# First layer's shift and scale columns on ScalarE, and the rope angles in three parts

## The reference

```python
c_act = jax.nn.silu(c)
shift, scale, gate = jnp.split(c_act @ mod_w[i] + mod_b[i], 3, axis=-1)
h = _rms_norm(x, norm_g[i]) * (1.0 + scale[:, None, :]) + shift[:, None, :]
q, k, v, g = jnp.split(h @ w_in, [RET_DK, 2 * RET_DK, 2 * RET_DK + RET_DV], axis=-1)
# _rope(q) and _rope(k), both with
ang = positions.astype(jnp.float32)[..., None, None] * inv
cos, sin = jnp.cos(ang), jnp.sin(ang)
return jnp.concatenate([x1 * cos - x2 * sin, x1 * sin + x2 * cos], axis=-1)
```

## Time and profile before

| | us |
|---|---|
| median of 3 runs | 722.12 |
| lowest and highest run | 721.81 and 723.71 |
| the profiled execution, its time | 723.09 |
| the profiled execution, its span | 721.3 |
| TensorE busy in the span | 704.7 |
| VectorE busy | 500.8 |
| ScalarE busy | 379.4 |

### The profile page before, as it was taken

How to read it: one execution, slowest core, us unless ns; L and a number is a source line. 1 busy time by engine, 2 the same in 40 slices (tenths; PEclk the granted TensorE clock), 3 DMA queues, 4 the chain that set the end, 5 groups by cost and what they waited for, 6 DMA issues and landing times.

```text
span 721.3 us, 9350 instructions
## 1 busy us (share of the span) xinstructions
PE 704.7 (98%) x3534; PEld 579.3 (80%) x3534; DVE 500.8 (69%) x727; ACT 379.4 (53%) x559; POOL 15.8 (2%) x33
## 2 busy tenths in 40 slices
PE   6999999999999999999999999999999999999996
PEld 5887877777888788788888888878888888888884
DVE  4699888787956778756668889955866545555444
ACT  5337543665645566554555755455565454444342
POOL 6000000000000000000000000000000000000000
PEclk8699999999999999999999999999999999999999
DMA  9998855667896166833454653333456655655511
GB/s 295 369 367 283 309 189 192 204 210 255 274 341 205 55 214 223 274 120 92 145 166 147 186 166 117 117 118 117 148 178 204 197 180 174 191 188 185 194 59 58
DMA packets 74476, 138.96 MB, mean 193 GB/s; under 512 B 5748, under 2 KB 18272, under 8 KB 74432
## 3 DMA queue, kind: packets, MB, share of 16 engines
q1 hardware_dynamic: 72816, 134.82, 57.4%
q10 hardware_dynamic: 736, 1.90, 0.7%
q0 software_dynamic: 880, 1.64, 0.6%
HBM read 137.31 MB, written 1.05 MB: 192 GB/s over the span
## 4 chain that ended last, share of the span: by engine, by line
PE 92%; DVE 4%; DMA 1%; issue 1%; ACT 1%; SPq 0%; DVEq 0%; ACTq 0%
PE G L382 24%; PE G L384 24%; PE G L383 23%; PE T L403 5%; PE T L771 2%; PE T L884 2%; PE T L761 1%; PE G L493 1%; DMA arena<-in_mod_w_dram 1%; PE G L494 1%; PE G L495 1%; DVE arena L1057 1%; DVE wlo L1057 1%; PE T L444 1%; DVE acc L1066 1%
## 5 line engine op out<-in xcount | busy, mean ns | idle before, releaser
L1057 DVE TENSOR_TENSOR wlo<-raw,whi 128x1024 fp32r<-128x1024 f32 x202 | 246.0, 1222 | 121.4 <-ACT whi L1805 120.9
L382 PE MATMUL G<-whi,ahi 128*128 128x512 f32 x760 | 307.5, 405 | 1.7 <-DVE wlo L1057 1.7
L384 PE MATMUL G<-whi,alo 128*128 128x512 f32 x760 | 297.2, 391 | 0.0
L383 PE MATMUL G<-wlo,ahi 128*128 128x512 f32 x760 | 296.3, 390 | 0.0
L1805 ACT ACTIVATE whi<-raw 128x1024 fp32r<-128x1024 f32 x202 | 212.9, 1060 | 124.1 <-PE G L384 108.9
L382 PEld LDWEIGHTS G<-whi,ahi 128*128 128x128 f32 x760 | 143.0, 188 | 32.2 <-DVE wlo L1057 4.1
L384 PEld LDWEIGHTS G<-whi,alo 128*128 128x128 f32 x760 | 142.7, 188 | 31.2
L383 PEld LDWEIGHTS G<-wlo,ahi 128*128 128x128 f32 x760 | 143.2, 188 | 28.0 <-issue 1.2
L1807 ACT ACTIVATE arena<-T,st 128x128 f32<-128x128 f32 (+2 forms) x56 | 21.6, 476 | 30.5 <-DVE st L1438 30.5
L403 PE MATMUL T<-head,arena 128*128 128x128 f32 x244 | 37.2, 277 | 0.0
L403 PEld LDWEIGHTS T<-head,arena 128*128 128x128 f32 x244 | 29.7, 141 | 9.2 <-issue 2.0
(11 more groups left out here) (227 smaller groups left out, 607.3 us busy)
## 6 DMA issues: line engine op xcount, KB each, us to landing
raw<-in_ret_w_in_dram SPq DMA_DIRECT2D x48, 512.0 KB, 5.6
raw<-in_w_gate_up_dram SPq DMA_DIRECT2D x40, 512.0 KB, 4.0
raw<-in_mod_w_dram SPq DMA_DIRECT2D x32, 512.0 KB, 4.9
raw<-in_fox_w_in_dram SPq DMA_DIRECT2D x32, 512.0 KB, 4.7
raw<-in_w_in_dram SPq DMA_DIRECT2D x28, 512.0 KB, 3.6
raw<-in_w_down_dram SPq DMA_DIRECT2D x22, 512.0 KB, 4.2
arena<-in_mod_w_dram SPq DMA_DIRECT2D x16, 512.0 KB, 8.3
raw<-in_ret_w_out_dram SPq DMA_DIRECT2D x16, 512.0 KB, 5.8
```

What stands on the lines that cost most here:

```text
L382: e.matmul(o, ah, wh, start=first and k == 0, stop=False)
L383: e.matmul(o, ah, wl, start=False, stop=False)
L384: done = e.matmul(o, al, wh, start=False, stop=last and k == 1)
L1057: e.tensor_tensor(o, a, b, op).then_inc(sig[name], 1)
```

## The change

`modulated(k)` goes from VectorE. Its two columns are made at the head of ScalarE's `x0_high(k)`, in two activations of one column each (Identity with scale and bias): shift is sum plus `mbc`, scale is `g_col` times sum plus a new column `mb1[:, 1]`, the product of `g_col` and `mb1[:, 0]`, which VectorE makes once for all eight blocks. `mod0` is now raised by ScalarE, which waits for it itself before it uses the columns. The `ring_to(1)` that stood ahead of `modulated(1)` goes too, as `ring_to(2)` follows. The three parts of the angles move into the loop: part k after `ring_to(u + 2)` of units 12, 13 and 14. No operation of the angles is changed, nor any transfer.

```diff
--- before.py
+++ after.py
@@ -195,7 +195,7 @@
         rows = sb("rows", [P, P])
         cols = sb("cols", [P, 44])
         mbc = sb("mbc", [P, 16])
-        mb1 = sb("mb1", [P, 8])
+        mb1 = sb("mb1", [P, 2, 8])
         cact = sb("cact", [P, 8])
         AB = sb("AB", [P, 2, 16])
         st = sb("st", [P, 80])
@@ -1126,13 +1126,6 @@
                     else:
                         stt(o, a, col(cact, r), o, ALU.mult, ALU.add, "macc" if last else "mod_sum")
 
-            def modulated(k):
-
-                on_.wait_ge(sig["sums"], k + 1)
-                on_.wait_ge(sig["columns"], 3)
-                tt(AB[:, 0, 8 + k:9 + k], sums_of(k, 0), mbc[:, k:k + 1], ALU.add, "mod0")
-                ts(AB[:, 0, k:k + 1], sums_of(k, 1), mb1[:, k:k + 1], g_col[:, 0, k:k + 1], ALU.add, ALU.mult, "mod0")
-
             def x0_low(k):
                 on_.wait_ge(sig["h_hi"], k + 1)
                 tt(alo[:, k, :], stage0[:, k % 4, :], ahi[:, k, :].bitcast(F32), ALU.subtract, "x0")
@@ -1146,16 +1139,15 @@
             t = T[bank_of["rows"]]
             copy(cols[:, 0:44], t[:, 8:52], "columns")
             copy(mbc[:, :], t[:, 54:70], "columns")
-            ts(mb1[:, :], t[:, 62:70], 1.0, None, ALU.add, None, "columns")
-            modulated(0)
+            ts(mb1[:, 0, :], t[:, 62:70], 1.0, None, ALU.add, None, "columns")
+            on_.wait_ge(sig["columns"], 3)
+            tt(mb1[:, 1, :], mb1[:, 0, :], g_col[:, 0, :], ALU.mult, "columns")
             ring_to(0)
             x0_low(0)
             copy(gains[:, 1:2], t[:, 53:54], "rows_read")
             ts(gains[:, 0:1], t[:, 52:53], 0.125, None, ALU.mult, None, "rows_read")
             tt(n1f[:, :], t[:, 70:78], n1_col, ALU.mult, "rows_read")
             mod_sums(1, 0, 4)
-            ring_to(1)
-            modulated(1)
             ring_to(2)
             x0_low(1)
             for g in (2, 3, 4):
@@ -1164,8 +1156,6 @@
                 ring_to(u - 1)
                 mod_sums(g, 4, 7)
                 ring_to(u)
-                modulated(k)
-                modulated(k + 1)
                 x0_low(k)
                 ring_to(u + 1)
                 x0_low(k + 1)
@@ -1249,12 +1239,12 @@
 
             u = 12
             ring_to(u)
-            for part in range(3):
-                angles(part)
             for c in range(4):
                 for k in range(4):
                     ring_to(u + 2)
                     u += 1
+                    if c == 0 and k < 3:
+                        angles(k)
                     if c == 3 and k >= 2:
                         scored(k - 2)
                 on_.wait_ge(sig["g"], done_at[u - 1, 1])
@@ -1880,6 +1870,10 @@
 
             def x0_high(k):
 
+                on_.wait_ge(sig["columns"], 4)
+                on_.wait_ge(sig["sums"], k + 1)
+                act(AB[:, 0, 8 + k:9 + k], sums_of(k, 0), ACT.Identity, "mod0", bias=mbc[:, k:k + 1])
+                act(AB[:, 0, k:k + 1], sums_of(k, 1), ACT.Identity, "mod0", scale=g_col[:, 0, k:k + 1], bias=mb1[:, 1, k:k + 1])
                 on_.wait_ge(sig["x0_turned"], k + 1)
                 on_.wait_ge(sig["mod0"], 2 * k + 2)
                 on_.wait_ge(sig["x0"], k - 3)
```

## The result

The changed kernel takes 723.46 us (median of 20 runs, 722.94 to 725.51), the kernel before 722.12 (20 runs, 721.29 to 723.92): 1.34 us slower, ratio 1.0021 with a 95% interval of 1.0014 to 1.0028. Forecast were 723.3 us and +1.2. The ratio lies inside the 0.3% in which the forecast put 0.79 of its chances, and the time inside its narrower forecast of 722.9 to 723.8.

What follows compares the result with a forecast made beforehand. TensorE, busy 704.7 of 721.3 us, was taken as the bound, with its few waits and a half-clock start. Columns −0.12 plus angles +1.31 gave +1.2 on 722.12: 723.3 us, range 721.1 to 725.0.

Steps and rivals of the forecast that it cites:

- Angles, +1.31: VectorE backlog, units 12 to 17: moved angles start unit 13 0.85 us earlier but the rope's first turning 1.31 later.
- The hole: VectorE idle 1.83 us before `wlo` 14, awaiting ScalarE's `whi` 14; rival that it doesn't open: 721.1 us, chance 0.16.
- upper bound of 1.6: Angles in the loop: if parts between other work cost 0.1 us more each, the loss is +1.6 us.
- The waits of TensorE: After the change, TensorE waits 0.6 us before unit 16 and 1.6 us before the rope's turning.
- Columns, −0.12: First gate: ScalarE's column pair lets `gate` start at 14.16 for 14.31; taken as −0.12 us.
- the nearest row is `cact`: Price of ScalarE's column pair, taken from an eight-column PSUM activation: 0.18 us, next activation starting 0.07 after it.
- The bound of two times 0.321: First gate, both activations at the trace's dearest small one, 0.321 us: `gate` at 14.53, +0.22 us.
- dear columns: Rival at the columns: small two-operand activations take 0.32 us, +0.22 for −0.12, giving 723.6 us; chance 0.10.
- The cover of the later pairs: Later groups: second pair queues behind ScalarE's `ahi`; block 3's `gate` 0.25 us later, covered by 0.3 us of slack.
- upper bound of +0.5: Whole columns part, forecast −0.12 us, between −0.2 and +0.5; lost cover of later pairs would be 0.3 us.
- The clock did not fall again: Rival: TensorE's waits before unit 16 and the rope's turning drop the clock to half, 729.8 us; chance 0.06.
- the fourth rival: Half clock at the start ends 3 us sooner or later than 28.9: ∓1.5 us, 721.8 or 724.8 us; chance 0.10.

Runs made afterwards that it cites:

- e2: Kernel before with only the angles moved into the loop, columns staying on VectorE; ratio 1.0025 (1.0011 to 1.0038), group's median 722.73 us beside before's 721.78.
- e1: Changed kernel with VectorE's loop as before, so only the columns move to ScalarE; ratio 1.0010 (0.9995 to 1.0024), group's median 722.33 us beside before's 721.78.
- e8: e1 with both bias columns left out and Copy in place of Identity, so the output differs; ran once, only its trace used, no time given.
- e4: Changed kernel with ScalarE making whi of unit 14 ahead of the two SiLUs; ratio 1.0006 (0.9992 to 1.0021), group's median 721.74 us beside before's 721.78.

## Why the prediction was right, and where it wasn't

- **Angles, +1.31.** The mechanism was right in each step, its size 0.38 us too large: e2 shows +0.93 in C and 0.95 in time. The term that was mis-sized is the angles' own. The step took the parts at their old spacing, 1.38, 1.33 and 1.33: between other work they take 1.25, 1.25 and 1.20 (68.17 to 69.42, 71.75 to 73.00 and 75.33 to 76.53 in e2), as nothing waits there for the result before. That is 0.34 of the 0.38. The hole's size is not in it: it was forecast at 1.83 and is 1.60, but only because the mod ahead of it ended later; `wlo` 14 starts at 67.02 in e2, and 67.05 was forecast. I had moved the cost the wrong way, too: the upper bound of 1.6 rested on parts that would get dearer. The waits of TensorE came out smaller with it, 0.43 for 0.6 and 1.3 for 1.6.
- **Columns, −0.12.** Wrong in sign. The step that failed is "the nearest row is `cact`": it has no operand columns. The trace of before had the better row: the two `fz` activations of 128x32, 0.229 us without an operand column and 0.321 with one. The bound of two times 0.321 gave +0.22 at the first gate, and A is longer by 0.22 to 0.23; that it fits so well is luck. It put `gate` 0.71 us after the sums (14.53 − 13.82), which is measured (16.14 − 15.43), but as 0.04 + 0.67, and it is 0.11 + 0.60: ScalarE starts later after the sums, and its pair overlaps. The rival "dear columns" (0.10) was right about this gate, and its sign, a `gate` at 14.4 or later, came; its 723.6 us left out the second place. Right with it was the rule of the Trainium skill ("ScalarE: Activation LUTs", section "Rules for kernel authors", about 0.3 us for an activation with a bias pointer): the traces have 0.26 and 0.34. The prediction held `cact` against it, but `cact` has no bias column.
- **The cover of the later pairs.** The step looked at block 3, whose lateness is hidden, and let it stand for all groups. At the last group there is no slack: before, `wlo` 11 starts at 57.20 just as both `alo` 7 and `whi` 11 are over (57.08 and 57.09), and from there VectorE has a backlog up to the rope, but for 0.17 us at unit 12. Alone that costs 0.34 us; beside the hole only 0.06. With A that makes +0.56 for the columns alone, just over the prediction's upper bound of +0.5. The 0.25 us that it counted as sooner for block 6 did not come: `gate` starts 1.59 us after the group's first sum in e1 (53.63 − 52.04) and 1.58 before (54.14 − 52.56).
- **The sum** was right by luck, by two errors of opposite sign: 1.31 − 0.12 = 1.19 forecast, and by the marks 0.99 (C) + 0.23 (A) = 1.22, with the 0.16 at block 1 1.38 in an execution whose clock is back to full by then. Measured are 1.34 us by the medians. Small slips in the prediction's arithmetic don't matter: 14.16 for 14.31 is −0.15 and not −0.12 (and has 0.20 where the row has 0.18), two full durations give −0.06 and not −0.05, and unit 16 is wanted at 75.2 and not 75.1.
- **The rivals.** The hole did open. The clock did not fall again near 75 to 80 us: D and the matmul spacing are as before. The half clock of the start does end elsewhere from run to run, as the fourth rival had it, but in both kernels. That the medians of 20 runs each even it out fully is assumed, not shown.

## What to carry to other kernels

Work that looks like a queue in front of an engine may be sitting in a hole: before moving it, ask what its engine would wait for if it were gone; here that was a `whi` which ScalarE makes behind two SiLUs and a table load. Of a backlog the last consumer counts, not the first: TensorE's wait of 0.74 us ahead of unit 13 went, and one of 1.3 us at the end of the same backlog came. And take the price of a small operation from a row with the same operands, and the slack of a repeated step at its last repetition.

## What the runs showed of the hardware

The operand columns of an activation cost about 0.09 us each in its duration (0.17, 0.26 and 0.34 us in e8 and e1), and a bias another 0.09 in the start of the one behind it (0.07 in e8, 0.16 in e1). And the record of the granted clock can miss a stretch at half speed. In the changed kernel's profile it is 1.00 from 18 to 20 us, while the matmuls start 0.43 us apart, the distance they had before 28.9 in the kernel before, and 0.23 apart from 23.3 on (e4's profile shows the same):

```profile
18.00:20.00 2.00, 2.00 (x5) 1.55 (x6) 1.89 (x5) 2.00 (x3) 0.00 (x0) 1.00 1.10 350
```

```profile
18.32 0.63 PE L494 MATMUL G<-wlo,ahi 128*128 128x512 f32 x1
18.75 0.63 PE L495 MATMUL G<-whi,alo 128*128 128x512 f32 x1
19.17 0.63 PE L493 MATMUL G<-whi,ahi 128*128 128x512 f32 x1
...
23.27 0.40 PE L494 MATMUL G<-wlo,ahi 128*128 128x512 f32 x1
23.50 0.40 PE L495 MATMUL G<-whi,alo 128*128 128x512 f32 x1
```

The first line is the stretch (PEclk is the third number from the end), the others TensorE's timeline. The mean granted clock of such a run, 0.997, says little of how long its start ran at half speed; the spacing of equal matmuls does.
